# Issuing the second table's rows ahead of the next step's first-table rows

## The reference

```python
def one_chunk(xc):                       # 128 tokens
    q = (xc @ wq).reshape(P_CHUNK, P_HEADS, 2, P_HALF)
    sc = jnp.einsum('thcd,hcnd->thcn', q, sub_keys)
    s1, i1 = lax.top_k(sc[:, :, 0], 16); s2, i2 = lax.top_k(sc[:, :, 1], 16)
    ...                                  # 16 best of the 256 pairs: top_s, eidx
    gate = jax.nn.softmax(top_s, axis=-1)
    u = jnp.take(u_tab, eidx, axis=0)    # rows of the first table
    act = jax.nn.gelu(jnp.einsum('thkd,td->thk', u, xc))
    vv = jnp.take(v_tab, eidx, axis=0)   # rows of the second table
    return jnp.einsum('thk,thkd->td', gate * act, vv)
```

## Time and profile before

| what | value |
|---|---|
| time of the kernel, median of 3 runs | 3092.7 us (3091.23 to 3098.33) |
| the profiled execution: span | 3171.0 us |
| the profiled execution: a time of its own beside the span | none recorded; the span is 78.3 us above the median |
| mean granted clock of TensorE | 0.870 |
| bytes moved by DMA | 961.85 MB, 303 GB/s over the span |
| of these by the gathers (queue q0) | 805.40 MB |

### The profile page before, as it was taken

One profiled execution on the slowest core, in us unless ns is written; L12 is line 12 of the kernel. 1 busy time (PEld: TensorE's weight loads), 2 busy tenths in 40 slices (PEclk: granted clock), 3 DMA queues, 4 the chain that ended last, 5 costly groups with the idle time before them and its releaser, 6 DMA issues.

```text
span 3171.0 us, 27910 instructions
## 1 busy us (share of the span) xinstructions
PE 2487.3 (78%) x6500; PEld 1148.6 (36%) x6500; DVE 1897.5 (60%) x5815; ACT 550.0 (17%) x1600; POOL 1712.9 (54%) x1588
## 2 busy tenths in 40 slices
PE   7875888788979888767788896789966766666667
PEld 1244333345623233323354343444732222222222
DVE  0044367873475657768757538784366777477664
ACT  0121112222111111112211112332111111111111
POOL 0002445443366667667667544463346777577675
PEclk9867899888989989888889798888988888778888
DMA  8526787667889999989999787776768999789888
GB/s 293 198 94 239 282 285 275 236 241 266 300 319 401 402 403 401 368 299 343 359 378 396 247 307 255 262 285 223 274 222 323 360 351 337 293 325 339 320 327 303
DMA packets 298730, 961.85 MB, mean 303 GB/s; under 512 B 28304, under 2 KB 30736, under 8 KB 297840
## 3 DMA queue, kind: packets, MB, share of 16 engines
q0 software_dynamic: 221184, 805.40, 69.5%
q1 hardware_dynamic: 77328, 154.96, 13.6%
q10 hardware_dynamic: 96, 0.10, 0.0%
HBM read 957.63 MB, written 2.62 MB: 303 GB/s over the span
## 4 chain that ended last, share of the span: by engine, by line
PE 39%; DVE 29%; issue 14%; DMA 9%; POOL 3%; ACT 2%; another core or an unknown queue 2%; DVEq 0%; POOLq 0%; SPq 0%; ACTq 0%
PE ps_acc L785 17%; DVE u_ring L1309 10%; PE ps_mm L610 5%; PE ps_mm L751 5%; DMA u_ring<-peer_u,gathered 4%; PE ps_mm L571 3%; PE ps_mm L723 2%; DMA v_ring<-peer_v,gathered 2%; POOL u_ring L517 2%; DMA weights<-ada_w 2%; POOL v_ring L517 2%; PE ps_mm L664 1%; DVE half_idx L1262 1%; DVE half_top L1258 1%
## 5 line engine op out<-in xcount | busy, mean ns | idle before, releaser
L785 PE MATMUL ps_acc<-v_ring,diag 128*128 128x512 f32 x3072 | 1536.5, 654 | 452.4 <-ACT diag L979 249.0
L517 POOL DMA_INDIRECT u_ring<-peer_u,gathered x768 | 836.3, 1089 | 795.0 <-DVE dots L1309 466.9
L785 PEld LDWEIGHTS ps_acc<-v_ring,diag 128*128 128x128 f32 x3072 | 626.6, 211 | 1279.1 <-issue 1052.5
L517 POOL DMA_INDIRECT v_ring<-peer_v,gathered x768 | 861.3, 1121 | 339.8 <-issue 216.0
L1309 DVE CUSTOM_DVE_ANT_0 u_ring<-u_ring,h 128x1024 f32<-128x1024 f32 x768 | 908.3, 1221 | 71.9 <-DMA u_ring<-peer_u,gathered 68.3
L979 ACT ACTIVATE diag<-consts,coef 128x128 f32<-128x128 f32 x768 | 245.6, 390 | 150.3 <-DVE coef L1323 87.0
L610 PE MATMUL ps_mm<-weights,hT 128*128 128x512 f32 x480 | 213.4, 598 | 2.9 <-DMA weights<-w_in 1.8
L1321 DVE TENSOR_SCALAR gexp<-gexp 128x4 f32<-128x4 f32 x192 | 41.6, 217 | 282.3 <-ACT gexp L973 216.0
L973 ACT ACTIVATE gexp<-poly 128x4 f32<-128x4 f32 x192 | 39.3, 205 | 891.8 <-DVE poly L1318 658.3
L751 PE MATMUL ps_mm<-hT,weights 128*128 128x128 f32 (+1 forms) x1024 | 182.6, 332 | 9.2 <-issue 8.6
L571 PE MATMUL ps_mm<-weights,condT 128*2 128x512 f32 x384 | 172.4, 605 | 18.3 <-DMA weights<-ada_w 18.3
(11 more groups left out here) (184 smaller groups left out, 1820.4 us busy)
## 6 DMA issues: line engine op xcount, KB each, us to landing
weights<-ada_w SPq DMA_DIRECT2D x24, 2048.0 KB
weights<-w_in SPq DMA_DIRECT2D x20, 2048.0 KB
weights<-peer_wq SPq DMA_DIRECT2D x16, 2048.0 KB
weights<-w_out SPq DMA_DIRECT2D x8, 2048.0 KB
u_ring<-peer_u,gathered POOLq DMA_INDIRECT x768
v_ring<-peer_v,gathered POOLq DMA_INDIRECT x768
weights<-peer_keys SPq DMA_DIRECT2D x4, 1024.0 KB
par<-params SPq DMA_DIRECT2D x2, 1026.0 KB
```

Of the source, the lines that this page charges most:

```text
L517: pool.indirect_dma_start(ring[:, slot, :], None, table, bass.IndirectOffsetOnAxis(ap=gathered[:, p, at:at + 1], axis=0)).then_inc(full[sl ...
L785: last = pe.matmul(ps_acc[:, b * NB:(b + 1) * NB], diag[:, slot, :], v_ring[:, slot, b * NB:(b + 1) * NB], start=False, stop=False)
```

## The change

In each step, POOL issues the four second-table gathers of the present step first, and after them the four first-table gathers of the next step. At the last step of a head they therefore come ahead of `take` too. No gather is added or removed, and each keeps its own wait. No other engine's program is touched.

```diff
             def head(n, p, last=False):
 
                 for g in range(STEPS):
+                    gather(v_ring, v_full, v_used, peer_v, n, p, g)
                     if g + 1 < STEPS:
                         gather(u_ring, u_full, u_used, peer_u, n, p, g + 1)
                     elif not last:
                         take(n + 1, 1 - p)
                         gather(u_ring, u_full, u_used, peer_u, n + 1, 1 - p, 0)
-                    gather(v_ring, v_full, v_used, peer_v, n, p, g)
```

## The result

The changed kernel takes 3114.06 us (median of 5, 3104.78 to 3121.97), the kernel before 3092.7 us in the same comparison. The ratio is 1.0064, 95% interval 1.0046 to 1.0081: slower, by some 20 us. The forecast was 3118. The rest of this document shows that the sum was right and the place was not.

A forecast was written before the change was run, and what follows sets the result against it. Transfers bound 951 to 1268 us, PE around 400 us, and DVE set the pace in the last two tiles. Terms of 21, 3 and 1 us gave +25 on the 3092.7 median: 3118 us, range 3078 to 3160.

The forecast's parts named there:

- The 1 us for the end of the kernel: Kernel end: u of the last step stands one group later, 5.0 us, costed at 1 (0 to 5).
- The shape: New trace, signs: POOL's v issues wait more for PE, PE's v-landing waits fall below 99.1 us, DVE's u waits rise.
- 14 x 1.5 = 21 us: Last two tiles: 14 heads with a search, each losing 1.5 us as DVE waits for u rows; 21 us.
- forecast of some 70 us: After 2345 us, a sign: POOL's v issues wait for PE 14 x 5 = 70 us or so, against 6.3 before.
- u1' is 2.0 us late: Worked head, last two tiles: the next head's step 1 u group starts at 2910.8 us instead of 2908.82.
- nobody waits for PE except the next v slot and the end of a tile: Last two tiles: DVE sets the pace, so issuing v rows at least 5.0 us earlier was costed at nothing.
- In 951 to 1268 the rows wait for transfers, not for their issue, and the total of bytes is the same.: 951 to 1268 us, DMA moving 402 GB/s: the change costs nothing there.
- + 3 us: 1310 to 1760 us: eight or so similar heads, background work hiding part of the loss; 3 us added.
- much slower: u landings are on the chain where DMA is full: 890 to 1310 us: 7 or 8 heads have u one group later, 35 us more, 3153 us; chance 0.16.
- Around 400 us ... it costs nothing: Around 400 us: u rows would still be 25 us ahead of their use, so no cost.
- `route` by chance: Search for the experts: its length varies, 13.3 or 21.0 us; three such shift 23 us either way; no chance given.
- faster: 890 to 1310 us: PE gets v rows in time, half of 63 us comes back, 31 us, giving 3062; chance 0.17.

The follow-up runs named there:

- second trace of before: The kernel before the change, unedited, traced again: 3098.37 us with a span of 3096.2, beside a median of 3098.85.
- first trace: The profile of the unedited kernel before the change that the prediction was read from: span 3171.0 us, median time 3092.7.
- the experiment with background chunks: PE's background chunks ahead of the four rows 0, 1, 1, 2 instead of 2, 1, 1, 0: old order 3309.58 us, new order 3384.97 us.

## Why the prediction was right in its sum and wrong in its place

The forecast of +25 us against a measured +21 is luck as far as the sum goes: 21 of the 25 were put where nothing was lost, and 24 us came from heads 8 to 23, for which it had 3. The 1 us for the end of the kernel isn't seen by itself. The mechanism was right, and it is in heads 8 to 23 that it costs time.

- *The shape.* v waits of PE vanish (293.0 us in the second trace of before, none listed after), u waits of DVE grow (135.8 to 259.4) and so do POOL's waits for PE: right.
- *"14 x 1.5 = 21 us" in the last two tiles.* This term failed. It measured -4.4 us between the traces, which is within the scatter of the table, and 0.9984 (0.9970 to 0.9997) alone. The wait of POOL for PE is there, but smaller than the forecast of some 70 us, and paid for: from 2321 us on in the second trace of before, POOL waits 25.6 us for DVE before u issues and 6.7 for PE before v issues; after, from 2349, 12.4 and 24.3. DVE waits 11.1 us more for u landings (117.7 to 128.8) and 10.8 us less at the ends of tiles, where PE's sum comes sooner (39.8 to 29.0). I had followed one head to the point where u1' is 2.0 us late and charged it to DVE, and then costed the earlier v rows at nothing, as "nobody waits for PE except the next v slot and the end of a tile". The end of the tile was worth about as much.
- *"In 951 to 1268 the rows wait for transfers, not for their issue, and the total of bytes is the same."* This step failed as well. Bytes are the same, but the rate fell from 398 to 381 GB/s over heads 8 to 15, and in a stretch that transfers bound nothing made that up. It lost 13.5 us, of which 0 was forecast.
- *"+ 3 us" in 1310 to 1760.* Mis-sized: heads 16 to 23 lost 10.5 us. The reason given for a small term was that background work hides part of the loss, but it is also what PE does while POOL waits for a slot. With the order changed at step 0 alone this stretch loses as much (10.3 us).
- *The rival "much slower: u landings are on the chain where DMA is full".* It named the place, and its argument against itself, "the queue there is never empty", was the wrong half. Its price, 35 us more, was too high: 13.5 us.
- *"Around 400 us ... it costs nothing."* Right: up to the end of the first tile the difference is 0.8 us.
- *"`route` by chance", 23 us either way.* The first trace had pauses that the executions timed at 3091 to 3098 us evidently didn't have. I took its 78.3 us over the median for a constant to subtract. It was a sign of this. The first trace also gave v landings 2% of the chain where the second gives 10%, so the price of the rival "faster", 31 us, was read from too low a share; what speaks against that rival is that u landings took the place of v landings.

What is shown: the place (heads 8 to 23 alone carry the cost), that PE's time on the rows is needed for it, that DVE waits for just the u groups that were moved back, and the DMA rate that falls in heads 8 to 15. What is argued only: that the lost transfers make up exactly the 13.5 us of heads 8 to 15, and that PE is late there because of background work; the experiment with background chunks doesn't settle that. The shares of single steps and parts rest on one trace each. Open: what ends the unnamed waits, why some comparisons have them and others don't, and why the new order has more of them.

No version is worth taking: the new order in the last two tiles alone gains 0.16% (0.03 to 0.30) where searches are short, and its variant at step 0 loses 1.9% where they are long. That variant where they are short is the one that would be worth measuring.

## What to carry to other kernels

An in-order issuer passes its wait on to everything behind it: here 12.03 us of waiting for one slot held a whole u group. Before two groups are swapped on it, ask of each wait how late its releaser can be in every stretch, not only in the one that is easiest to follow; where transfers are the bound, the question is whether the queue still holds work when the wait ends. And if the span of a trace is far from the median of the times, take a second trace before reasoning from single microseconds of the first.

## What the runs showed of the hardware

The same kernel took 3099 and 3090 us in two comparisons and 3177 and 3201 us in two others, 2.5 to 3.6% apart. Each of the four was taken on another chip (3 and 10, then 0 and 5), so chip and time can't be told apart here (that of the first trace of before isn't recorded). In the traces of the slower two, DVE waits on its own previous instruction for up to 7.0 us at a time during the search, and ACT and POOL have waits with no named releaser as well, of up to 17.1 and 4.9 us; in those of the faster two there is none. What the order of POOL's issues costs goes with it: the same edit costs 0.64% in the one case and 2.6% in the other.

POOL's issue of a gather takes 0.94 us, and 1.4 to 2.0 us where DVE runs dot products. The Trainium skill, "SBUF — State Buffer", section "Who interferes with whom", has a DVE instruction with two inputs in SBUF and a GpSimd instruction that reads SBUF exclude each other for a whole instruction. The traces agree for the dot products, which read `u_ring` and `h`: the 1.98 us at 1175.19 in the changed kernel, beside a dot product that starts at 1175.15, are 1.04 more than 0.94, which is less than one dot product's 1.22. No run here ties the pauses in the search to that rule: in the first trace of before POOL issues at 0.94 us through the search of 13.3 us, and just so through the one of 21.0 us before it (from 2873.00 to 2890.12).
